# Six of 80 projection tiles of an fp32r matmul streamed with other column counts

## The reference

```python
proj = jnp.einsum('btd,dc->btc', x, w_in)
u_pre, v_pre, q_pre, f_pre, i_pre, g_pre, gate_a, gate_b = jnp.split(proj, _split_points(), axis=-1)
y_a, v_rows = chunk_spatial_gating(u_pre, v_pre, sgu_ln_g, sgu_ln_b, w_s, b_s)
y_b, S_new = hgrn2_mix(q_pre, f_pre, i_pre, g_pre, lb, hgrn_norm_g, S0)
merged = jax.nn.sigmoid(gate_a) * (y_a @ w_out_a) + jax.nn.sigmoid(gate_b) * (y_b @ w_out_b)
x = layer_norm(ALPHA * x + merged @ w_o, ln1_g, ln1_b)
x = layer_norm(ALPHA * x + moe_ffn(x, router_w, router_b, w_gate, w_up, w_down), ln2_g, ln2_b)
```

## Time and profile before

| | |
|---|---|
| median of the timed executions | 1679.07 us (1678.76 and 1679.37) |
| span of the profiled execution | 1674.8 us |
| what lies around the span | about 4.3 us |
| TensorE busy | 1603.3 us (96%), 10500 matmul records |
| TensorE weight loads busy | 1070.9 us (64%) |
| mean granted TensorE clock | 0.997 |
| DMA moved | 543.80 MB, mean 325 GB/s |

### The profile page before, as it was taken

One profiled execution on the slowest core, in us unless ns is written; L12 is line 12 of the kernel. 1 busy time (PEld: TensorE's weight loads), 2 busy tenths in 40 slices (PEclk: granted clock), 3 DMA queues, 4 the chain that ended last, 5 costly groups with the idle time before them and its releaser, 6 DMA issues.

```text
span 1674.8 us, 24058 instructions
## 1 busy us (share of the span) xinstructions
PE 1603.3 (96%) x10500; PEld 1070.9 (64%) x10500; DVE 694.8 (41%) x1039; ACT 392.8 (23%) x419; POOL 45.9 (3%) x85
## 2 busy tenths in 40 slices
PE   8999999999999999999999988998998899889998
PEld 8999999999999999983533422424334234225324
DVE  7447678658585575554611110111021011103726
ACT  7444555623454332330000000000000000000002
POOL 2000000012000000000000000000000000000000
PEclk9999999999999999999999999999999999999998
DMA  9675465589656759879999999999999999999995
GB/s 265 187 209 167 132 190 164 160 219 324 192 155 182 246 176 309 273 289 396 426 429 427 428 428 428 429 428 429 428 430 427 430 428 428 429 427 429 427 419 201
DMA packets 252800, 543.80 MB, mean 325 GB/s; under 512 B 6416, under 2 KB 219488, under 8 KB 228656
## 3 DMA queue, kind: packets, MB, share of 16 engines
q1 hardware_dynamic: 245632, 524.93, 83.1%
q0 software_dynamic: 4896, 15.49, 2.9%
q10 hardware_dynamic: 2192, 2.20, 0.4%
HBM read 535.65 MB, written 6.95 MB: 324 GB/s over the span
## 4 chain that ended last, share of the span: by engine, by line
PE 75%; DMA 23%; DVE 1%; ACT 1%; issue 0%; SPq 0%; DVEq 0%; ACTq 0%
PE bank L640 12%; PE bank L641 12%; PE bank L642 12%; PE bank L938 12%; PE bank L1032 11%; DMA ring_high<-wu 11%; DMA ring_low<-wu 9%; PE bank L912 5%; PE bank L1110 3%; DMA ring_low<-w_in 2%; PE bank L685 1%; DMA ring_high<-wd 1%; PE bank L1018 0%; PE bank L1104 0%; PE bank L955 0%
## 5 line engine op out<-in xcount | busy, mean ns | idle before, releaser
L642 PE MATMUL bank<-x_hi,w_lo 128*128 128x264 f32 x1216 | 344.7, 284 | 0.0
L640 PE MATMUL bank<-x_hi,w_hi 128*128 128x264 f32 x1200 | 343.9, 287 | 0.0
L641 PE MATMUL bank<-x_lo,w_hi 128*128 128x264 f32 x1200 | 340.4, 284 | 0.0
L1412 DVE TENSOR_TENSOR w_lo<-ring_low,w_hi 128x2048 fp32r<-128x2048 f32 x107 | 244.8, 2289 | 145.1 <-ACT w_hi L1216 144.5
L938 PE MATMUL bank<-ring_low,reg_pk 128*64 128x512 f32 x1136 | 254.6, 596 | 29.6 <-DMA ring_low<-wu 24.8
L1216 ACT CAST w_hi<-ring_low 128x2048 fp32r<-128x2048 f32 x107 | 203.7, 1904 | 141.9 <-PE bank L642 86.6
L642 PEld LDWEIGHTS bank<-x_hi,w_lo 128*128 128x128 f32 x1216 | 228.1, 188 | 0.0
L640 PEld LDWEIGHTS bank<-x_hi,w_hi 128*128 128x128 f32 x1200 | 226.3, 189 | 1.8 <-issue 1.7
L938 PE MATMUL bank<-ring_high,reg_pk 128*64 128x512 f32 x896 | 201.0, 596 | 26.8 <-DMA ring_high<-wu 26.8
L641 PEld LDWEIGHTS bank<-x_lo,w_hi 128*128 128x128 f32 x1200 | 226.4, 189 | 0.1
L938 PEld LDWEIGHTS bank<-ring_low,reg_pk 128*64 128x64 f32 x1136 | 77.9, 137 | 200.5 <-issue 146.2
(11 more groups left out here) (383 smaller groups left out, 1766.5 us busy)
## 6 DMA issues: line engine op xcount, KB each, us to landing
ring_high<-wd SPq DMA_DIRECT2D x40, 2048.0 KB, 33.7
ring_low<-w_in SPq DMA_DIRECT2D x76, 1024.0 KB, 5.8
ring_low<-wg SPq DMA_DIRECT2D x38, 2048.0 KB, 35.3
ring_low<-wu SPq DMA_DIRECT2D x33, 2048.0 KB, 27.9
ring_high<-wu SPq DMA_DIRECT2D x30, 2048.0 KB, 26.8
ring_high<-wg SPq DMA_DIRECT2D x26, 2048.0 KB, 35.3
ring_low<-wd SPq DMA_DIRECT2D x22, 2048.0 KB, 32.7
ring_low<-wo SPq DMA_DIRECT2D x16, 1024.0 KB, 7.0
```

The lines of the kernel that those rows point to most:

```text
L640: pe.matmul(out, hi[k], of_hi[:, k, :], start=(k == 0), stop=False)
L641: pe.matmul(out, hi[k], of_lo[:, k, :], start=False, stop=False)
L642: mm = pe.matmul(out, lo[k], of_hi[:, k, :], start=False, stop=(k == kk - 1))
L1412: dve.tensor_tensor(lo_of(q), raw_of(q), hi_of(q).bitcast(F32), ALU.subtract).then_inc(lo_ready, 1)
```

## The change

Tiles 70 to 75 are streamed otherwise, the other 74 as before.

- Tiles 70, 71 and 72 (WIDER) move 272, 288 and 296 columns in place of 264. The input is read as one flat row of 16 x 264 words, so the columns past 264 are the first of the next chunk's rows; their products land in columns 264 and up of the bank, which nobody reads. The last chunk, which has no successor, keeps 264. So 45 of a tile's 48 matmuls are wider.
- Tiles 73, 74 and 75 (SPLIT) move the same 264 columns in two parts: 256 + 8, 248 + 16 and 128 + 136. The first part goes through all 16 chunks, then the second does. A tile has 96 matmuls in place of 48, and 96 weight loads.

```diff
+WIDER = {70: 272, 71: 288, 72: 296}
+SPLIT = {73: 256, 74: 248, 75: 128}
...
+            def wider_tile(n, hi, lo, width):
+
+                pe.wait_ge(act_evac, n - 3)
+                hi_row, lo_row = (w[:, :, :].rearrange("p k t -> p (k t)") for w in (x_hi, x_lo))
+                for k in range(KD):
+                    some = width if k < KD - 1 else T
+                    out, cols = psum[n % 4][:, 0:some], slice(T * k, T * k + some)
+                    pe.matmul(out, hi[k], hi_row[:, cols], start=(k == 0), stop=False)
+                    pe.matmul(out, hi[k], lo_row[:, cols], start=False, stop=False)
+                    mm = pe.matmul(out, lo[k], hi_row[:, cols], start=False, stop=(k == KD - 1))
+                mm.then_inc(gemm, 1)
+
+            def split_tile(n, hi, lo, first):
+
+                pe.wait_ge(act_evac, n - 3)
+                for cols in (slice(0, first), slice(first, T)):
+                    out = psum[n % 4][:, cols]
+                    for k in range(KD):
+                        pe.matmul(out, hi[k], x_hi[:, k, cols], start=(k == 0), stop=False)
+                        pe.matmul(out, hi[k], x_lo[:, k, cols], start=False, stop=False)
+                        mm = pe.matmul(out, lo[k], x_hi[:, k, cols], start=False, stop=(k == KD - 1))
                 mm.then_inc(gemm, 1)
...
-                gemm_tile(n, [hi[:, k, :] for k in range(KD)], [lo[:, k, :] for k in range(KD)], x_hi, x_lo)
+                parts_hi, parts_lo = ([w[:, k, :] for k in range(KD)] for w in (hi, lo))
+                if n in WIDER:
+                    wider_tile(n, parts_hi, parts_lo, WIDER[n])
+                elif n in SPLIT:
+                    split_tile(n, parts_hi, parts_lo, SPLIT[n])
+                else:
+                    gemm_tile(n, parts_hi, parts_lo, x_hi, x_lo)
                 side(n)
```

## The result

The changed kernel took 1709.7 us (1708.76 and 1710.64), the kernel before 1679.07: a ratio of 1.0191, 95% interval 1.0174 to 1.0208, 30.6 us slower by the medians. It lies outside the range of the prediction, 1688 to 1704, and above its 1695.5. The profiled execution of the changed kernel took 1708.76 us for a span of 1707.0: 1.8 us lie around the span, and 1.7 to 1.9 in every run of the experiments. So the 4.3 us in the table of the kernel before are not what lies around the span; by 1.8 the profiled execution of the kernel before took some 1676.6 us (an estimate) and was not one of its two timed ones.

A forecast was written before the change was run, and what follows sets the result against it. The projection was taken as bound by TensorE's own matmul stream, the experts by weight transfers. Splits 15.2 plus wide tiles 1.2 gave 16.4; 1674.8 + 16.4 + 4.3 = 1695.5 us, range 1688 to 1704.

The forecast's parts named there:

- The shift to the end: Microseconds added to tiles 70 to 75 move the DMA-bound expert part as a whole, one for one to the end.
- The wide tiles: Tiles 70 to 72: 2880 more columns at 2.4 GHz cost 1.2 us, or 0.1 if loads set the pace.
- a fixed 10.8: Projection matmuls: each step is streaming plus a fixed 10.8 ns, never under 112 ns.
- The price of the splits at full clock: Tiles 73 to 75: 48 more matmuls and loads each cost 5.2 + 5.1 + 5.0 = 15.2 us.
- fp32r loads have the floor of fp32 loads: Split tiles' small parts: a full weight load every 109 to 112 ns, whatever the columns, as in fp32 rows.
- The clock falls: Rival: small parts of tiles 73 and 74 lower the clock, up to 14 us more; 1703, 1698 to 1710; chance 0.07.
- Four passes below 256 columns: Rival: in five split parts fp32r runs as plain fp32, 42 to 53 us more, 1721 to 1732; chance 0.14.
- Nearly free matmuls: Rival: small matmuls of split tiles take 74 ns or less, 7.9 us in all, 1688; chance 0.05.
- Full hiding of the delay: Rival: the delay in tiles 70 to 75 hides behind the DMA-bound regime; chance 0.02, given for a part hidden.
- Theory A: From the experiments: step is streaming plus 11 to 14 ns, at least 112, doubled at half clock; few-column parts lower the clock.

The follow-up runs named there:

- padded224: The changed kernel with every part under 224 columns widened to 224 by columns not read, last chunk excepted; ratio 1.0094 to the kernel before.
- after_again: The changed kernel as it is, run once more on the same chip; ratio 1.0195 to the kernel before.
- spread: The changed kernel without wide tiles, splits 256+8, 248+16, 128+136 moved to tiles 70, 74, 78 with plain tiles between; ratio 1.0128 to the kernel before.
- plain_between: The changed kernel with the 128+136 split at tile 76 instead of 75, a plain tile before it; ratio 1.0144 to the kernel before.
- padded64: The changed kernel with parts under 64 columns widened to 64 by columns not read, last chunk excepted; 1712.15 us, run once.
- Reorder: The changed kernel with the split tiles in another order: 128+136 in tile 73, 256+8 in 74, 248+16 in 75; ratio 1.0137 to the kernel before.
- alternating: The changed kernel with both parts of split tiles taken in turn, chunk by chunk, second part's rows left out of the result; ratio 1.0091 to the kernel before.
- halves_only: The kernel before with only tile 75 changed, split as 128+136; ratio 1.0028 to the kernel before.
- padded128: The changed kernel with parts under 128 columns widened to 128 by columns not read, last chunk excepted; 1692.36 us, run once.

## Why the prediction was wrong

**The shift to the end was right.** Tiles 70 to 75 are on TensorE's own path, and 32.9 us there moved the DMA-bound part unshortened.

**The wide tiles were right**: forecast 1.2 us, 6.26 + 6.33 + 6.48 us against 5.99 + 5.80 + 5.80 are 1.5. Columns set the pace; the addition is not a fixed 10.8 but 12.6 ns at 288 and 296 columns, (6.48 - 3 x 0.121)/45 - 0.1233 for the latter.

**The price of the splits at full clock was right**: forecast 15.2 us. In padded224, at full clock, tiles 73 to 75 take 10.96, 10.89 and 10.75 us against 5.80 each, 15.2. The steps, forecast as 117.5, 114.1 and 112 for 256, 248 and small, are 118, 115 and 110 to 112; errors of up to 2 ns that nearly cancel in the sum. That fp32r loads have the floor of fp32 loads, read from L901 and the like lengths of the loads, held.

**The step that failed** is the one that gave "The clock falls" a chance of 0.07 and left it out of the sum, because from 735 to 739 us "it stayed at 1.00". The prediction itself said that these were "a dozen small matmuls and not 48", and then priced the unknown by them. Nor does this place keep the clock each time. In four of the fourteen traces (after_again, spread, plain_between, padded64) the clock falls just behind it, within a microsecond of the start of the gather matmuls (L943; L912 in the kernel before), for 3.4 us. In after_again there are 17 records in that time, where the kernel before has 30 at 1.00 in as long:

```profile
772.80:776.20 3.40, 3.40 (x17) 0.50 1.01 426
```

So the trace before showed one of two outcomes of this place. Both traces of the changed kernel have two falls in these tiles, and its six timed executions lie between 1707.6 and 1712.4 us. Reorder and spread show that the stretch alone does it, alternating and the two wider paddings that mixing or widening takes it away.

**The rival was also mis-sized.** It counted two parts, up to 14 us, 7 likely. The clock's share in the changed kernel is tile 73 12.27 - 10.96 = 1.3 us, tile 74 14.46 - 10.89 = 3.6, tile 75 20.53 - 10.67 = 9.9, tile 76 7.32 - 5.85 = 1.5: **16.2 us**. 6.4 of it is the rival as worked out. The 9.9 in tile 75 are what it had not: that 128+136 columns, which would have kept a full clock, also keep a half clock. halves_only, reorder, spread and plain_between have this tile at 1.00 in 10.7 us; the changed kernel, its repetition and padded64, where it stands directly behind a fall, at 0.50 in 20.5. So what counts is the clock on arrival. 1.5 + 15.2 + 16.2 = 32.9, the shift of y_parts. The measured 1709.7 lies just within this rival's 1698 to 1710, and that is luck: its upper end stood for both small parts wholly at half clock, which no trace shows, and not for tile 75.

**Four passes below 256 columns** (1721 to 1732) missed by 11 us or more and was wrong in kind, though it has a place that fits: tile 75's steps of 214 ns are just about what it would give for 128 columns (216), and only the granted clock beside them, and the same matmuls at 110 ns in halves_only, tell the two apart. **Nearly free matmuls** fell with the floor of 111.5 ns. Full hiding of the delay fell with the unshortened rest.

**What stays open**: why the step has 11 ns beside its columns at 256 and more with more of them (15 ns at 384, some 20 at 512). It is not a fixed price, and Theory A's "all of it twice as long at half clock" holds for the load alone. In tile 76, at half clock, 264 columns step 220 ns, which is streaming at 1.2 GHz with nothing on top:

```profile
544.43 0.42 PE L643 MATMUL bank<-x_lo,w_hi 128*128 128x264 f32 x1
544.65 0.42 PE L644 MATMUL bank<-x_hi,w_lo 128*128 128x264 f32 x1
```

Open is also at which matmul the clock falls in a given execution; it came after 3.8 us of the 8-column part in one trace and after its end in another.

## What to carry to other kernels

Where each matmul loads 128 weight columns, at full clock the columns under some 240 are not worth saving, and a split costs a load, 111.5 ns, however small the part. Don't let parts of few columns stand in a row: take them by turns with the wide parts, or widen them with columns nobody reads, as a stretch of them costs the clock, and the following work of middling size may not give it back. When steps come out at double, read the granted clock of that window before looking for a rule in the sizes.

## What the runs showed that wasn't expected

- A matmul of 128 or 136 columns with a full load held the clock at the level it found, 1.00 in six traces (spread, halves_only, reorder, alternating, plain_between, padded128) and 0.50 in three (the changed kernel, its repetition, padded64), for 20.5 us; in every trace the clock came back in the first tile of 264 columns behind a fall, or before it in the part of 248 (from 513.2 us in the changed kernel).
- The step that the loads set follows the granted clock: 112 ns at 1.00 and 213 at 0.50, with 8 columns as with 136. The Trainium skill, "TensorE: Matmul & The Clock Gate", "LDWEIGHTS (loading the stationary operand)", gives columns over 1.2 GHz, an estimated 106.7 ns for 128, without the clock; at half clock the trace has twice that.
- Streaming 27,360 columns more (padded224) took 15 us off the changed kernel's loss.
